# The window cache's rows go to the output from memory to memory, during the first MLP instead of out of the attention's buffers

## What is computed

```
cache_win_kv (8, 512, 2, 4, 64)   # past keys and values of the window branch
shared, win_pos, new_cmp, new_sel, new_win = shared_kv(h, start, past_cmp, past_sel, past_win, ...)
win_rows = jnp.concatenate([past_win, new_win], axis=1)      # 512 old rows + 8 new ones
s_win_kv = win_rows[:, win_rows.shape[1] - n_keep:]          # the last 512 go out
```

## Time and profile before

| | us |
|---|---|
| median of 3 runs | 2373.51 |
| lowest and highest run | 2367.35, 2375.34 |
| span of the profiled execution | 2372.5 |
| TensorE busy | 2189.5 (92%) |
| GpSimd busy | 860.4 (36%) |
| VectorE busy | 849.7 (36%) |
| ScalarE busy | 652.3 (27%) |
| moved by the DMA engines | 184.57 MB, 78 GB/s on average |
| share of the 16 DMA engines: SP's queue, GpSimd's queue | 17.7%, 4.9% |

### The profile page before, as it was taken

One profiled execution on the slowest core, in us unless ns is written; L12 is line 12 of the kernel. 1 busy time (PEld: TensorE's weight loads), 2 busy tenths in 40 slices (PEclk: granted clock), 3 DMA queues, 4 the chain that ended last, 5 costly groups with the idle time before them and its releaser, 6 DMA issues.

```text
span 2372.5 us, 37626 instructions
## 1 busy us (share of the span) xinstructions
PE 2189.5 (92%) x15160; PEld 1989.3 (84%) x15160; DVE 849.7 (36%) x1839; ACT 652.3 (27%) x1105; POOL 860.4 (36%) x528
## 2 busy tenths in 40 slices
PE   7999999969879999999999997999899989999996
PEld 6988888859679999999899995665567979999995
DVE  7474747564332200121221216655321342002213
ACT  3442424322123211221231304433211242112212
POOL 2444444455246513553443230000000345435531
PEclk9998989889899989999999898999966989999998
DMA  4112112131221243222213331000442112222221
GB/s 159 65 50 104 52 63 81 45 127 47 87 71 62 81 102 103 80 83 86 97 54 140 107 90 54 1 1 1 137 165 72 62 45 80 80 80 80 80 84 54
DMA packets 53394, 184.57 MB, mean 78 GB/s; under 512 B 7070, under 2 KB 11838, under 8 KB 50720
## 3 DMA queue, kind: packets, MB, share of 16 engines
q1 hardware_dynamic: 41424, 138.05, 17.7%
q0 software_dynamic: 9568, 41.69, 4.9%
q10 hardware_dynamic: 2288, 3.23, 0.4%
HBM read 158.20 MB, written 27.28 MB: 78 GB/s over the span
## 4 chain that ended last, share of the span: by engine, by line
PE 73%; DVE 12%; issue 7%; ACT 4%; POOL 3%; ACTq 0%; DMA 0%; POOLq 0%; DVEq 0%
PE dense L1122 47%; PE dense L1375 3%; PE bS L1228 2%; PE bS L1293 2%; PE bM L1459 2%; DVE tile L1591 1%; PE dense L1411 1%; PE dense L1474 1%; POOL split L622 1%; PE bX L1459 1%; PE bS L1197 1%; DVE tile L1654 1%; POOL xs L715 1%; PE bS L1411 1%; PE dense L1532 1%
## 5 line engine op out<-in xcount | busy, mean ns | idle before, releaser
L1122 PE MATMUL dense<-xs,split 128*128 128x288 f32 x6848 | 986.4, 302 | 41.1 <-POOL xs L715 21.9
L1122 PEld LDWEIGHTS dense<-xs,split 128*128 128x128 f32 x6848 | 953.2, 193 | 57.1 <-issue 46.8
L622 POOL TENSOR_TENSOR split<-ring,split 128x1024 fp32r<-128x1024 f32 x212 | 543.4, 2564 | 892.1 <-ACT split L833 892.1
L833 ACT ACTIVATE split<-ring 128x1024 fp32r<-128x1024 f32 x212 | 225.0, 1061 | 894.8 <-PE dense L1122 880.3
L1122 PE MATMUL dense<-hid,split 128*128 128x288 f32 x3072 | 420.3, 299 | 5.8 <-POOL split L622 5.8
L1122 PEld LDWEIGHTS dense<-hid,split 128*128 128x128 f32 x3072 | 419.5, 192 | 6.1 <-POOL split L622 6.1
L1603 DVE SCALAR_TENSOR_TENSOR tile<-tile,dense 128x576 f32 (+1 forms) x56 | 42.2, 754 | 491.2 <-PE dense L1122 491.2
L1746 DVE TENSOR_SCALAR sq<-dense 128x576 f32<-128x576 f32 x64 | 48.5, 758 | 320.5 <-PE dense L1122 314.4
L808 POOL DMA_DIRECT2D o_win<-tile x8 | 4.6, 571 | 375.4 <-DMA tile<-in_win 375.4
L726 POOL TENSOR_TENSOR hid<-sq,hid 128x576 f32 x64 | 76.8, 1201 | 0.0
L1591 DVE SCALAR_TENSOR_TENSOR tile<-tile,tile,tile 128x512 f32<-128x512 f32 x72 | 71.8, 997 | 2.6
(11 more groups left out here) (301 smaller groups left out, 2530.0 us busy)
## 6 DMA issues: line engine op xcount, KB each, us to landing
ring<-in_w SPq DMA_DIRECT2D x212, 512.0 KB, 3.2
tile<-in_state POOLq DMA_DIRECT2D x4, 2048.0 KB, 9.4
o_sssm<-tile POOLq DMA_DIRECT2D x4, 2048.0 KB, 7.5
tile<-in_cmp POOLq DMA_DIRECT2D x32, 256.0 KB, 3.3
tile<-in_sel SPq DMA_DIRECT2D x32, 256.0 KB, 3.0
tile<-in_win SPq DMA_DIRECT2D x8, 1024.0 KB, 7.3
o_win<-tile POOLq DMA_DIRECT2D x8, 1024.0 KB, 4.2
o_kv<-tile POOLq DMA_DIRECT2D x1, 3456.0 KB, 12.7
```

The costliest lines, as they stand in the source:

```text
L622: pool.tensor_tensor(split[:, j, 1, :], ring[:, j, :], split[:, j, 0, :].bitcast(F32), ALU.subtract).then_inc(w_split, 1)
L833: act.activation(split[:, j, 0, :], ring[:, j, :], ACT.Copy).then_inc(w_hi, 1)
L1122: mm = pe.matmul(dense[:, 2 * par + h_, 0:HT], split[:, j, w, cols], v[:, kk, h_ * HT:(h_ + 1) * HT], start=kk == 0 and t == 0, stop=kk == ...
```

## The change

The eight stores out of the buffers go, with the semaphores `win_stored`, the helper `windows_stored`, and every wait on them. Instead GpSimd issues eight transfers from the input `in_win` straight to the output `o_win`, one for each sequence: three after `x_los(0)`, three between the two halves of the MLP, two behind it, ahead of the load of `in_cw1`. One semaphore, `win_kept`, counts them, and only GpSimd waits for it, before the output product of the attention. SP still loads the window rows for the attention.

```diff
-        win_stored = [sem(f"window_rows_stored{i}") for i in range(KVB)]
+        win_kept = sem("window_rows_kept")
...
-        def windows_stored(eng):
-            for i in range(KVB):
-                eng.wait_ge(win_stored[i], 16 * len(range(i, NB, KVB)))
...
                     sp.wait_ge(no_done, b - KVB + 1)
-                    sp.wait_ge(win_stored[b % KVB], 16 * (b // KVB))
...
+            def keep_windows(first, last):
+
+                for b in range(first, last):
+                    pool.dma_start(a["o_win"][b, :, :, :], a["win"][b, :, :, :]).then_inc(win_kept, 16)
...
             x_los(0)
+            keep_windows(0, 3)
             mlp_los(0, 0, S_M1[0][1] + 2)
+            keep_windows(3, 6)
             mlp_los(0, 1, S_KV + 2)
+            keep_windows(6, NB)
...
-            for b in range(NB):
-
-                pool.wait_ge(kv_loaded[b % KVB], 80 * (b // KVB + 1))
-                pool.dma_start(a["o_win"][b, :, :, :], wkv[b % KVB]).then_inc(win_stored[b % KVB], 16)
-            windows_stored(pool)
+            pool.wait_ge(win_kept, 16 * NB)
...
-            windows_stored(act)
...
-            windows_stored(dve)
```

## The result

| | before | changed |
|---|---|---|
| median of 20 runs, us | 2373.37 | 2378.17 |
| lowest and highest, us | 2367.35, 2380.99 | 2372.32, 2385.32 |
| ratio to before | | 1.0023, 95% interval 1.0013 to 1.0032 |
| span of the profiled execution, us | 2372.5 | 2383.6 |

The change costs 4.8 us by the medians, 0.23% by the ratio. That is slower, but inside the 0.3% that I had set as the bound of what is told from no change. The two profiled executions are 11.1 us apart, more than twice the difference of the medians, so they must be compared stage by stage and not by their ends.

What follows compares the result with a forecast made beforehand. TensorE carries most of the chain, fed by a two-slot ring. Terms 1.4 + 8.2 + 1.7 = 11.3 us (0 to 19.7), laid on 2372.5 or 2373.51, gave 2384 to 2385 us; range 2371 to 2398.

Steps and rivals of the forecast that it cites:

- the likeliest case: Whole kernel: the forecast of a slower kernel, 2379.5 to 2397 us, chance 0.46.
- rival 1: Whole kernel: transfers hidden after all, TensorE never stands for the ring, only third group left; 2373 to 2379 us, chance 0.40.
- the third group: Last two transfers, ahead of in_cw1 in GpSimd's queue: in_cw1 lands 10.5 us later, cost 1.7 us (0 to 3.5).
- my three signs of being wrong: Groups of three under 13 us; ring loads beside them landing within 12 us; the decode stage (attention) shrinking.
- the first group: Three transfers at 721.4 us: ring load lands at 739.5, may land by 738.1; cost 1.4 us.
- the second group: Three transfers between the MLP halves, 961.3 us: TensorE stands 6.0 us, loses 2.2 to the clock; cost 8.2 us.
- my two main terms: Delays of TensorE: second group between the MLP halves 8.2 us, third group ahead of in_cw1 1.7 us.
- What the change takes away: Decode attention: eight GpSimd stores of 0.53 us, one of SP's two waits, guards already met; gain 0.
- The issues: GpSimd's issuing of the eight transfers, 0.53 us each, hidden in its waits and gaps.
- How long they take: Memory-to-memory transfers at 200 GB/s, bounds 170 and 397: 15.7 us for three, 10.5 us for two.
- The upper bound: Transfer rate of 397 GB/s, reached by a store into memory with a ring load beside it.
- Who gets the DMA engines: Queues take turns by rows, not bytes: a ring load beside three 64 KB pieces per engine lands after nearly all.

## Why the prediction was right, and where it was not

**The direction and the range** (2371 to 2398) held. The point, 2384, was 6 us too high, and the likeliest case, slower by over 0.3%, did not come about: the time lies in what I called rival 1, "only the third group is left, 0 to 3.5 us", and the third group did cost 3.5. Of my three signs of being wrong the first came: three transfers were down 12.9 us after the first issue, so they moved data for less than the 13 us I had named, not for 15.7. Of the second, the ring load beside the first group was in time (8.7 us) and that beside the second was not (12.6). For the third, one profile can't tell the attention within 1 us. That the range held is in part its width, since it took in the forecast and rival 1 alike; that the direction held hangs on the smaller of my two main terms.

**What the change takes away** was counted as 0. Right as far as it can be measured: without any store the ratio is 1.0001, within 0.0013.

**The issues** were hidden, as said: 0.5 us each, in GpSimd's idle stretches.

**How long they take** is the term that was mis-sized, and the others followed from it. I took 200 GB/s, near the only transfer from memory to memory in the trace; it is 357 with pieces of 64 KB and 359 with pieces of 4 KB, ring loads included. The upper bound, taken from the store of `o_kv`, was nearly the truth. Why bskew is slower stays open: I had blamed its short rows, and did not weigh that it reads the same rows over and over and goes through another queue. Rows of 1.5 KB reached 330 GB/s, but in packets of three. The Trainium skill's 207 to 214 GB/s (DMA: Bandwidth & Descriptors, Latency and other measured facts) is for rows a wide pitch apart. It does not carry over to these copies, whose pieces lie one behind the other and which ran at 357, and the measurement decides.

**Who gets the DMA engines**, by turns and not by bytes, was right, as the pair of runs with long and short pieces shows. One row for one piece was too strict: the ring got nearly three rows on each engine between two pieces. With three transfers the load still lands only after nearly all of them, as I had said.

**First group:** 1.4 us expected, none found. The ring load landed in 8.7 us, not 13. I had misread o_kv's start, on which this leaned: its data began 2.4 us after the issue and not 1.2. It did no harm, since the first group's own began after 1.2 us.

**Second group:** 8.2 us expected, 0.9 found. It was the largest term. The ring load took 12.6 us, not 17.9; with the 2.6 us spare behind ScalarE's turn, which I had worked out, TensorE stood 0.51 us. So the step failed by the rate: six transfers at once gave the stand of 5.92 us with the fallen clock that I had put at three.

**Third group:** 1.7 us expected, between 0 and 3.5; 3.5 found, although the transfers were faster than assumed. Two errors stood against each other; that the cost still came out within its range is luck. `in_cw1` was late by 5.1 us and not by 10.5. But my 4 us of free time rested on the sums taking 9.02 us, as in the profile of before, half of them at full clock. After a wait of 3.6 to 3.9 us they run wholly at 1.2 GHz and take 13.8 us (10.5 after a wait of 1.3), and the first pieces of the next product run at half clock too. I had charged that loss in the second group and forgotten it in the third. And I took TensorE's place in time from one profile, in which the clock had already made it over 2 us late; where it was not late, the same two transfers cost 5.4 us. By the Trainium skill (TensorE: Matmul & The Clock Gate, Part 1: The HAM clock gate) the clock drops after idling and returns with sustained work. The drop to 0.82 and then 0.50 in the stand agrees; the some 17 us at half clock that follow, nearly all with TensorE busy, are shown by the windows above.

## What to carry to other kernels

A transfer off the critical path can cost time by what is queued behind it: look first for the next load in the same queue that somebody waits for, and issue that one ahead. Where two queues share the DMA engines, the length of a piece in one sets how long the other waits; cutting 64 KB pieces to the neighbours' 4 KB cost nothing in rate here (359 against 357 GB/s) and took the stand away. Price a delay of TensorE with the clock that follows it, not only with the idle time, and take the time at which TensorE is ready from several profiles. And count a queue's packets before comparing the speed of two transfers by the length of their rows.

## What the hardware showed unexpectedly

- Copies from memory to memory reached 357 GB/s in pieces of 64 KB, 359 in pieces of 4 KB and 330 in rows of 1.5 KB, each with ring loads beside. The rows of 1.5 KB went some three to a packet. The 170 GB/s of bskew stayed the exception, unexplained.
- The granted clock fell to 1.2 GHz with TensorE busy. In the profile of the kernel without window stores TensorE is busy without a gap from 1184 to 1196, and these rows of its windows span the position sums:

```profile
1178.00:1184.00 6.00, 6.00 (x38) 1.00 0.00 0
1184.00:1190.00 6.00, 6.00 (x35) 0.60 0.01 3
1190.00:1196.00 6.00, 6.00 (x29) 0.55 0.00 0
1196.00:1202.00 6.00, 5.36 (x34) 1.00 0.00 0
```

  The position sums are 64 matmuls of one column each, 0.14 to 0.22 us apart. In every one of the 13 profiles at least their last part ran at 1.2 GHz, with or without a wait ahead of them.
